# Expert jobs in pairs: 128 places in three passes, then 64 places in two

## The chip, the cores and the metric

The kernel runs on one core of a Trainium2 chip, in one launch. The metric is the device time of that launch in microseconds. Four compute engines matter: TensorE (PE in the profile, its weight loads PEld), VectorE (DVE), ScalarE (ACT) and GpSimd (POOL). SyncE (SP) issues the loads.

## The reference

The reference is a decoder trunk of two layers on 256 tokens of width 1024: an mLSTM layer with a dense SwiGLU, then a sparse attention layer with a mixture of experts, and a last RMSNorm. All is float32. The part that matters here is the mixture:

```python
logits = (t @ w_router)
top_v, top_i = lax.top_k(logits, TOP_K)               # 2 of 8 experts for each token
gate = sum(one_hot(top_i) * softmax(top_v))
gu = einsum('nd,edf->nef', t, w_gu)                   # 1024 -> 2 * 3584 for each expert
act = silu(gu[..., :3584]) * gu[..., 3584:] * gate[..., None]
out = einsum('nef,efd->nd', act, w_down)              # 3584 -> 1024
```

With 256 tokens and two experts each, 512 places are to be filled. On the inputs of the reference its router chooses experts 0 to 7 for 48, 41, 94, 73, 60, 101, 42 and 53 tokens.

## The kernel before

Weights come as slots of 1 MB (128 partitions x 2048 float32), in the order of use: 71 slots for everything ahead of the mixture, then 42 for each expert (28 for gate and up, 14 for down). They pass a ring of 7 raw slots (`RAW`). For float32 precision with the faster fp32r matmul each slot is split: ScalarE copies it to `w_hi` (rounded), VectorE writes `w_lo = raw - w_hi`. Both have a ring of 3 (`SPLIT`). The activations are split in the same way, and TensorE adds three products in `mm3` (lines 1136 to 1138): high x high, high x weight-low, low x weight-high.

So a slot n moves along a chain. SP loads it when VectorE has done slot n-7. ScalarE makes `w_hi` (line 627) when TensorE has used slot n-3. VectorE makes `w_lo` (line 1082). TensorE uses it in 12 matmuls of 128x512 and increments `s_used`. Every engine runs its own instruction list in order, and semaphores tie the lists together.

The mixture runs as jobs in a hardware loop (`Fori(0, jobs)`), one job for each expert with room for 128 places, plus a further job for each expert with more than 128 tokens; with the counts above that is 8 jobs. In a job:

- `gather` (line 1499) picks the tokens of the expert with a one-hot matrix, `gather_t` (line 1514) transposes them, `places` (lines 1505, 1507) makes the gate of each place and the matrix for the way back. They are done for the next job in the down phase of this one.
- Seven chunks of four slots make 512 of the 3584 inner columns each: slots 0 and 1 the gate half in bank 0, slots 2 and 3 the up half in bank 1. ScalarE takes the SiLU into `sg` (line 645), VectorE multiplies with the gate and the up half into `av` (line 1101). In the next chunk `job_t` (line 1547) transposes `av` in four matmuls, ScalarE makes `at_hi` (line 632) and VectorE `at_lo` (line 1089).
- Fourteen down slots accumulate the output in banks 2 and 3. Then `y_hi` (line 661), `y_lo` (line 1112), the scatter back to token order (lines 1594, 1595) and four additions into the residual `xs` (line 1120).

ScalarE and VectorE work `AHEAD` = 2 slots ahead of TensorE in a job, and `TURN` = 3 slots into the next. The table of jobs is made by VectorE ahead of the loop (lines 1033 to 1062), and TensorE, ScalarE, VectorE and SP read the count of jobs from it.

## Time and profile before

| | us |
|---|---|
| median of three runs | 1585.07 (1583.67 to 1586.74) |
| profiled execution, its own time | 1586.67 |
| its span in the profile | 1584.9 |
| TensorE busy | 1536.5 (97%) |
| VectorE busy | 1213.0 (77%) |
| ScalarE busy | 1038.5 (66%) |
| mean load rate over the span | 274 GB/s |

The span runs from the first to the last instruction of the profiled execution. "Idle before" in a row is the time that the engine waited ahead of such instructions, and what ended it. A matmul's duration includes the time in which the next is already running, so the distance between two starts tells the pace, and not the duration.

### The profile page before, as it was taken

The numbers are of one execution on the slowest core, as the hardware profiler recorded it, in microseconds if no ns is written. First come the engines' busy times: TensorE is split into PE (matmuls) and PEld (weight loads), VectorE is DVE, ScalarE is ACT, GpSimd is POOL, SyncE is SP. The second block draws the span as 40 slices with busy tenths as digits, with TensorE's granted clock in tenths as the row PEclk, the third lists the DMA queues.
The fourth block names the chain that finished last, engine by engine and source line by source line (L and its number), as shares of the span: only waits on it lengthen the run. The fifth ranks groups of instructions, "written<-read, shape, count | busy, mean of one in ns | idle before, by whom it ended". The sixth has DMA issues, their size and how long they took to land.

```text
span 1584.9 us, 20492 instructions
## 1 busy us (share of the span) xinstructions
PE 1536.5 (97%) x7380; PEld 1256.4 (79%) x7380; DVE 1213.0 (77%) x1051; ACT 1038.5 (66%) x1006; POOL 38.4 (2%) x92
## 2 busy tenths in 40 slices
PE   7998999999999979999999999999999999999997
PEld 7986888879944668888888887887887887888886
DVE  5945555457458478888988989888988888988887
ACT  5544444346447457777777777777777777777775
POOL 6000000010000000000000000000000000000001
PEclk9998999999959989999999999999999999999999
DMA  8542555535500229989999998998999999998994
GB/s 332 188 158 106 186 187 186 184 134 188 211 1 1 93 102 361 373 329 369 361 348 363 365 352 330 370 360 336 365 360 332 375 351 343 363 365 339 365 359 169
DMA packets 60091, 434.19 MB, mean 274 GB/s; under 512 B 6672, under 2 KB 6672, under 8 KB 7568
## 3 DMA queue, kind: packets, MB, share of 16 engines
q1 hardware_dynamic: 59904, 433.09, 72.5%
q8 instruction: 27, 0.44, 0.1%
q10 hardware_dynamic: 144, 0.52, 0.1%
q14 instruction: 16, 0.13, 0.0%
HBM read 432.54 MB, written 1.05 MB: 274 GB/s over the span
## 4 chain that ended last, share of the span: by engine, by line
PE 93%; DVE 3%; ACT 2%; issue 1%; POOL 0%; DMA 0%; DVEq 0%; POOLq 0%; ACTq 0%
PE bank L1136 27%; PE bank L1138 27%; PE bank L1137 27%; PE bank L1421 2%; PE bank L1447 2%; PE bank L1547 2%; DVE w_lo L1082 1%; PE bank L1499 1%; PE bank L1431 1%; PE bank L1401 1%; PE bank L1449 1%; ACT ht_hi L385 1%; PE bank L1514 0%; DVE w_lo L677 0%; PE bank L1594 0%
## 5 line engine op out<-in xcount | busy, mean ns | idle before, releaser
L1082 DVE TENSOR_TENSOR w_lo<-raw,w_hi 128x2048 fp32r<-128x2048 f32 x336 | 763.3, 2289 | 116.2 <-ACT w_hi L627 115.2
L627 ACT ACTIVATE w_hi<-raw 128x2048 fp32r<-128x2048 f32 x336 | 644.9, 1920 | 161.6 <-PE bank L1138 161.6
L1136 PE MATMUL bank<-w_hi,ht_hi 128*128 128x512 f32 (+1 forms) x1252 | 489.6, 391 | 7.8 <-DVE w_lo L1082 6.1
L1138 PE MATMUL bank<-w_hi,ht_lo 128*128 128x512 f32 (+1 forms) x1252 | 482.9, 386 | 0.0
L1137 PE MATMUL bank<-w_lo,ht_hi 128*128 128x512 f32 (+1 forms) x1252 | 482.4, 385 | 0.0
L1136 PEld LDWEIGHTS bank<-w_hi,ht_hi 128*128 128x128 f32 x1252 | 236.4, 189 | 57.1 <-DVE w_lo L1082 9.6
L1138 PEld LDWEIGHTS bank<-w_hi,ht_lo 128*128 128x128 f32 x1252 | 236.2, 189 | 47.7
L1137 PEld LDWEIGHTS bank<-w_lo,ht_hi 128*128 128x128 f32 x1252 | 236.6, 189 | 44.9
L677 DVE TENSOR_TENSOR w_lo<-raw,w_hi 128x2048 fp32r<-128x2048 f32 x73 | 166.5, 2288 | 128.6 <-ACT w_hi L358 128.6
L358 ACT ACTIVATE w_hi<-raw 128x2048 fp32r<-128x2048 f32 x73 | 139.6, 1919 | 117.1 <-PE bank L1138 116.9
L1136 PE MATMUL bank<-w_hi,at_hi 128*128 128x512 f32 x536 | 211.1, 394 | 0.0
L1138 PE MATMUL bank<-w_hi,at_lo 128*128 128x512 f32 x536 | 209.1, 390 | 0.0
L1137 PE MATMUL bank<-w_lo,at_hi 128*128 128x512 f32 x536 | 208.7, 389 | 0.0
L1138 PEld LDWEIGHTS bank<-w_hi,at_lo 128*128 128x128 f32 x536 | 100.6, 188 | 21.3
L1137 PEld LDWEIGHTS bank<-w_lo,at_hi 128*128 128x128 f32 x536 | 100.8, 188 | 20.2
L1136 PEld LDWEIGHTS bank<-w_hi,at_hi 128*128 128x128 f32 x536 | 100.7, 188 | 20.0
L1136 PE MATMUL bank<-ht_hi,w_hi 128*128 128x256 f32 x256 | 74.2, 290 | 2.7 <-DVE w_lo L677 2.5
L1138 PE MATMUL bank<-ht_hi,w_lo 128*128 128x256 f32 x256 | 73.4, 287 | 0.0
L1137 PE MATMUL bank<-ht_lo,w_hi 128*128 128x256 f32 x256 | 73.4, 287 | 0.0
L645 ACT ACTIVATE sg<-bank 128x512 f32<-128x512 f32 x56 | 33.5, 599 | 42.4 <-PE bank L1138 42.3
L1136 PEld LDWEIGHTS bank<-ht_hi,w_hi 128*128 128x128 f32 x256 | 50.2, 196 | 3.9 <-DVE w_lo L677 2.7
L1137 PEld LDWEIGHTS bank<-ht_lo,w_hi 128*128 128x128 f32 x256 | 50.2, 196 | 0.0
(260 smaller groups left out, 1154.0 us busy)
## 6 DMA issues: line engine op xcount, KB each, us to landing
raw<-in_moe SPq DMA_DIRECT2D x339, 1024.0 KB, 6.9
raw<-in_wts SPq DMA_DIRECT2D x71, 1024.0 KB, 4.8
xs<-in_x SPq DMA_DIRECT2D x2, 512.0 KB, 3.7
out<-xn SPq DMA_DIRECT2D x2, 512.0 KB, 2.7
pk<-in_packed SPq DMA_DIRECT2D x1, 517.0 KB, 6.4
g1b<-in_norm_ffn ACTq DMA_DIRECT2D x1, 512.0 KB, 6.6
gfb<-in_norm_final SPq DMA_DIRECT2D x1, 512.0 KB, 3.7
```

Of the source, the lines that this page charges most:

```text
L358: a(w_hi[:, n % SPLIT, :], raw[:, n % RAW, :], ACT.Copy).then_inc(s_hi, 1)
L385: a(ht_hi[:, k, :], B[banks[b]][:, (k % 2) * 256:(k % 2) * 256 + 256], ACT.Copy, scale=pk[:, C_GAIN + 8 * gain + k:C_GAIN + 8 * gain + k + ...
L627: a(w_hi[:, n % SPLIT, :], raw[:, n % RAW, :], ACT.Copy).then_inc(s_hi, 1)
L645: a(sg[:, 0, :], B[0][:, :], ACT.Silu).then_inc(s_silu, 1)
L677: v.tensor_tensor(w_lo[:, n % SPLIT, :], raw[:, n % RAW, :], w_hi[:, n % SPLIT, :].bitcast(F32), ALU.subtract).then_inc(s_lo, 1)
L1082: v.tensor_tensor(w_lo[:, n % SPLIT, :], raw[:, n % RAW, :], w_hi[:, n % SPLIT, :].bitcast(F32), ALU.subtract).then_inc(s_lo, 1)
L1136: mm(out_, sh, mh, start=first, stop=False)
L1137: mm(out_, sh, ml, start=False, stop=False)
L1138: return mm(out_, sl, mh, start=False, stop=last)
L1421: mm(B[n % 3][:, 0:2 * lk], qt[lo:lo + 64, h // 2, t * P:(t + 1) * P], kt[lo:lo + 64, :, h // R, 0:lk], start=True, stop=True).then_inc(s_ ...
L1447: mm(bank[0:64, :], vv[:, k, b, g * DB:(g + 1) * DB], ptg[grp % 2][:, j, :, :] .rearrange("p r q -> p (r q)"), start=j == 0, stop=False)
L1547: ins = nc.tensor.transpose(B[4 + c % 2][:, j * P:(j + 1) * P], av[:, 0, j * P:(j + 1) * P], ident[:])
```

## The change

Jobs come in pairs. The first of a pair (kind 0) has 128 places and works in three passes as before. The second (kind 1) has 64 places. Its stationary matrix holds the high parts of 64 tokens in columns 0 to 63 and their low parts in columns 64 to 127, so that two matmuls take the place of three: with `w_hi` and with `w_lo`. Rows 0 to 63 of the product are the high part's share and rows 64 to 127 the low part's. They are added by `folded_t`: in place of four transposes of `av`, eight float32 matmuls with a 128x64 matrix `fold` (two identities on top of each other) transpose the gate half and the up half and add the two shares. For that ScalarE copies both halves out of the banks (`sg`, `av`), takes the SiLU after the fold (`silu_t`) and makes the high part (`high_b`), and VectorE multiplies (`product_t`) and makes the low part (`low_b`). ScalarE and VectorE split slots in another order in kind 1, with less lead.

The gate is no longer multiplied in at `av` but at the end of a job, in `y_hi` (a scale for each row) and `y_lo`.

Experts 1 to 7 are sorted by their count. Expert 0 and the three with the highest counts take the jobs of 128 places, the four with the lowest those of 64. A further pair of jobs is made for each expert that has more tokens than its job has places. The table for that is longer; VectorE makes it in the first job, behind the second chunk's product (`job_tables`). The first pair of jobs is written out ahead of the loop, which starts at pair 1. The number of slots and of bytes loaded for each job stays as it was.

```diff
-NJ_MAX = 11
 JOB_SLOTS = 7 * 4 + 14
+PAIRS, PAIRS_MAX = NE // 2, NE // 2 + 4
+CAP_B = 64
...
+    def at_job(i, k, per, plus):
+
+        return i * (2 * per) + (k * per + plus)
...
             load(n, wts[n, :, :])
-        with sp.Fori(0, NE) as i:
+        for s in range(JOB_SLOTS):
...
+        def expert_loads(i, k):
+            if isinstance(i, int):
+                e = sp.value_load(tab[0:1, 1 + 2 * i + k:2 + 2 * i + k], min_val=0, max_val=NE - 1)
+            else:
+                e = sp.value_load(tab[0:1, bass.ds(i * 2 + (1 + k), 1)], min_val=0, max_val=NE - 1)
             for s in range(JOB_SLOTS):
-                load(N0 + s, job_slot(bass.ds(i, 1), s), 1, i * JOB_SLOTS)
-        sp.wait_ge(s_tab, 1)
-        jobs = sp.value_load(tab[0:1, 0:1], min_val=NE, max_val=NJ_MAX)
-        with sp.If(jobs > NE):
-            with sp.Fori(NE, jobs) as i:
-                e = sp.value_load(tab[0:1, bass.ds(i - (NE - 1), 1)], min_val=0, max_val=NE - 1)
-                for s in range(JOB_SLOTS):
-                    load(N0 + s, job_slot(bass.ds(e, 1), s), 1, i * JOB_SLOTS)
+                load(N0 + s, job_slot(bass.ds(e, 1), s), 1, at_job(i, k, JOB_SLOTS, 0))
+
+        expert_loads(0, 1)
+        with sp.Fori(1, pairs) as i:
+            expert_loads(i, 0)
...
+            def silu_t(c):
+                act.wait_ge(s_tp, at_job(i, kind, 7, 11 + c + 1))
+                a(sgt[:, c % 2, :], B[4 + c % 2][:, 0:4 * CAP_B], ACT.Silu).then_inc(s_sgt, 1)
+
+            def high_b(c):
+                act.wait_ge(s_avt, i * 7 + (c + 1))
+                a(at_hi[:, 4 * c * P:(4 * c + 4) * P].rearrange("p (k t) -> p k t", k=4)[:, :, 0:CAP_B],
+                  avt[:, c % 2, :].rearrange("p (k t) -> p k t", k=4), ACT.Copy).then_inc(s_tph, 1)
+
+            split(TURN)
+            if not (isinstance(i, int) and kind == 0):
+                act.wait_ge(s_scat, at_job(i, kind, 4, 0))
+            act.wait_ge(s_gs, at_job(i, kind, 1, 1))
             a(gcol[:], B[6][:, 2 * P:2 * P + 1], ACT.Copy).then_inc(s_gc, 1)
-            split(TURN)
-            act.wait_ge(s_xu, i * 4 + 12)
             a(selt[:], B[6][:, 0:2 * P], ACT.Copy).then_inc(s_sgc, 1)
...
+                    split(4 * c + 3)
+                    if c:
+                        silu_t(c - 1)
+                    used(4 * c + 1)
+                    if c >= 2:
+                        act.wait_ge(s_tp, at_job(i, kind, 7, 11 + c - 1))
+                    a(sg[:, c % 2, :], B[0][:, :], ACT.Copy).then_inc(s_silu, 1)
+                    split(4 * c + 4)
+                    if c:
+                        high_b(c - 1)
+                    split(4 * c + 5)
+                    used(4 * c + 3)
+                    a(av[:, c % 2, :], B[1][:, :], ACT.Copy).then_inc(s_mul, 1)
+                split(28 + 3)
+                silu_t(6)
+                split(28 + 4)
+                high_b(6)
...
+            act.wait_ge(s_gc, at_job(i, kind, 1, 1))
...
-                a(y_hi[:, h * 512:(h + 1) * 512], B[2 + h][:, :], ACT.Copy).then_inc(s_yh, 1)
+                    used(JOB_SLOTS - 1)
+                a(y_hi[:, h * 512:(h + 1) * 512], B[2 + h][:, :], ACT.Copy, scale=gcol[:, 0:1]).then_inc(s_yh, 1)
...
+        def one_hot(j, cap=P):
             for t in range(NT):
-                v.tensor_tensor(sel_oh[:, t, :], slot_iota[:], posj[:, t, j].broadcast_to([P, P]),
+                iota = slot_iota[:, 0:cap].rearrange("p (o n) -> p o n", o=1).broadcast_to([P, P // cap, cap])
+                pos = posj[:, t, j].rearrange("p (o n) -> p o n", o=1).broadcast_to([P, P // cap, cap])
+                v.tensor_tensor(sel_oh[:, t, :].rearrange("p (o n) -> p o n", n=cap), iota, pos,
                                 ALU.is_equal).then_inc(s_sel, 1)
...
+        def job_tables():
...
+            step(v.tensor_tensor(above, above, tie, ALU.add))
+            step(v.tensor_reduce(order, above, AX.X, ALU.add))
+            v.tensor_scalar(large, order, 4.5, None, ALU.is_gt).then_inc(s_dc, 1)
+            v.tensor_scalar(number, order, 2.0, -1.0, ALU.mult, ALU.add).then_inc(s_dc, 1)
+            ch[0] += 2
+            step(v.tensor_scalar(order, order, 0.0, None, ALU.is_equal))
+            step(v.scalar_tensor_tensor(number, large, -7.0, number, ALU.mult, ALU.add))
...
+            step(v.tensor_tensor(large, large, order, ALU.add))
+            step(v.tensor_scalar(cap, large, float(P - CAP_B), float(CAP_B), ALU.mult, ALU.add))
+            step(v.tensor_tensor(over, cnt, cap, ALU.is_gt))
...
+            def spread(table, src, first, n, cols):
+                pick = picks[:, first:first + n, :].rearrange("p (o k) e -> p o k e", o=1).broadcast_to([P, NT, n, NE])
+                work = pwork[:, :, 0:n, :]
+                step(v.tensor_tensor(work, pick, src.rearrange("p t (o e) -> p t o e", o=1)
+                                     .broadcast_to([P, NT, n, NE]), ALU.mult))
+                step(v.tensor_reduce(table[:, :, cols], work, AX.X, ALU.add))
...
+            def product_t(c):
+                dve.wait_ge(s_sgt, i * 7 + (c + 1))
+                if c >= 2:
+                    dve.wait_ge(s_tph, at_job(i, kind, 7, 11 + c - 1))
+                    dve.wait_ge(s_tpl, at_job(i, kind, 7, 11 + c - 1))
+                v.tensor_tensor(avt[:, c % 2, :], sgt[:, c % 2, :], B[4 + c % 2][:, 4 * CAP_B:8 * CAP_B],
+                                ALU.mult).then_inc(s_avt, 1)
+
+            def low_b(c):
+                dve.wait_ge(s_avt, i * 7 + (c + 1))
+                dve.wait_ge(s_tph, at_job(i, kind, 7, 11 + c + 1))
+                both = at_hi[:, 4 * c * P:(4 * c + 4) * P].rearrange("p (k t) -> p k t", k=4)
+                v.tensor_tensor(both[:, :, CAP_B:P], avt[:, c % 2, :].rearrange("p (k t) -> p k t", k=4),
+                                both[:, :, 0:CAP_B].bitcast(F32), ALU.subtract).then_inc(s_tpl, 1)
+
+            if kind == 0:
...
+            else:
+                for c in range(7):
+                    split(4 * c + 2)
+                    if c:
+                        product_t(c - 1)
+                    split(4 * c + 3)
+                    if c:
+                        low_b(c - 1)
+                    split(4 * c + 5)
...
+                product_t(6)
+                split(28 + 4)
+                low_b(6)
+                split(28 + 4 + AHEAD)
...
+                dve.wait_ge(s_yh, at_job(i, kind, 2, h + 1))
+                v.scalar_tensor_tensor(y_lo[:, h * 512:(h + 1) * 512], B[2 + h][:, :], gcol[:, 0:1],
+                                       y_hi[:, h * 512:(h + 1) * 512].bitcast(F32), ALU.mult, ALU.subtract).then_inc(s_yl, 1)
             split(JOB_SLOTS - 1 + AHEAD)
...
-                          kk == 0, kk == 7)
+                if kind == 0:
+                    lo = ht_lo[:, kk // 2, (kk % 2) * P:(kk % 2) * P + P]
+                    ins = mm3(bank[:, :], hi, lo, weights(w_hi, n, 512)[:, k, :], weights(w_lo, n, 512)[:, k, :],
+                              kk == 0, kk == 7)
+                else:
+                    mm(bank[:, :], hi, weights(w_hi, n, 512)[:, k, :], start=kk == 0, stop=False)
+                    ins = mm(bank[:, :], hi, weights(w_lo, n, 512)[:, k, :], start=False, stop=kk == 7)
             ins.then_inc(s_used, 1)
...
+            def folded_t(c):
+                pe.wait_ge(s_silu, at_job(i, kind, 7, 12 + c + 1))
+                pe.wait_ge(s_mul, at_job(i, kind, 7, 12 + c + 1))
+                if c >= 2:
+                    pe.wait_ge(s_avt, i * 7 + (c - 1))
+                for half, src in enumerate((sg, av)):
+                    for j in range(4):
+                        to = (4 * half + j) * CAP_B
+                        ins = mm(B[4 + c % 2][:, to:to + CAP_B], src[:, c % 2, j * P:(j + 1) * P], fold[:],
+                                 start=True, stop=True)
+                ins.then_inc(s_tp, 1)
...
-                    pe.wait_ge(s_silu, i * 7 + 12 + c)
-                    gu(4 * c, B[0], i)
-                gu(4 * c + 1, B[0], i)
+                    pe.wait_ge(s_silu, at_job(i, kind, 7, 12 + c))
+                    gu(4 * c, B[0], i, kind)
+                    if kind:
+                        folded_t(c - 1)
+                gu(4 * c + 1, B[0], i, kind)
                 if c:
-                    job_t(c - 1)
-                    pe.wait_ge(s_mul, i * 7 + 12 + c)
+                    if kind == 0:
+                        job_t(c - 1)
+                    pe.wait_ge(s_mul, at_job(i, kind, 7, 12 + c))
...
+                            ins = mm3(B[2 + half][:, :], hi, at_lo[:, kk * P:(kk + 1) * P],
+                                      weights(w_hi, n, 1024)[:, k, w], weights(w_lo, n, 1024)[:, k, w], first, last)
+                        else:
+                            mm(B[2 + half][:, :], hi, weights(w_hi, n, 1024)[:, k, w], start=first, stop=False)
+                            ins = mm(B[2 + half][:, :], hi, weights(w_lo, n, 1024)[:, k, w], start=False, stop=last)
                     if d == 13 and half == 0:
...
+        job(0, 0)
+        job(0, 1)
+        pe.wait_ge(s_tab, 1)
+        pairs = pe.value_load(tab[0:1, 0:1], min_val=PAIRS, max_val=PAIRS_MAX)
+        with pe.Fori(1, pairs) as i:
+            job(i, 0)
+            job(i, 1)
 
```

## Rows read from the trace of the kernel before

**Rows 1.** First section of the page.

```profile
PE 1536.5 (97%) x7380; PEld 1256.4 (79%) x7380; DVE 1213.0 (77%) x1051; ACT 1038.5 (66%) x1006; POOL 38.4 (2%) x92
```

**Rows 2.** Windows; columns: length, busy time of each engine, granted clock, DMA share, GB/s.

```profile
6.00:32.00 26.00, 22.18 (x155) 21.23 (x156) 17.96 (x24) 13.04 (x19) 20.24 (x49) 0.93 1.01 416
588.00:1570.00 982.00, 975.75 (x4453) 805.59 (x4452) 860.71 (x520) 738.35 (x521) 0.00 (x0) 1.00 0.92 351
```

**Rows 3.** The tile selt: one such copy in each job.

```profile
L640 ACT ACTIVATE selt<-bank x8: 360/385/388, 584.1 to 1451.7; 128x256 fp32r<-128x256 f32 x8
```

**Rows 4.** Timeline of TensorE in a chunk; columns: start, duration in us, what.

```profile
1019.25 0.39 PE L1136 MATMUL bank<-w_hi,ht_hi 128*128 128x512 f32 x1
...
1025.14 0.39 PE L1138 MATMUL bank<-w_hi,ht_lo 128*128 128x512 f32 x1
1025.37 0.60 PE L1547 MATMUL bank<-ident,av 128*128 128x128 f32 x4
1025.72 0.47 PE L1136 MATMUL bank<-w_hi,ht_hi 128*128 128x512 f32 x1
```

**Rows 5.** Groups by line and shape, window 620 to 1540 (busy us, mean ns, idle before).

```profile
L1082 DVE TENSOR_TENSOR w_lo<-raw,w_hi 128x2048 fp32r<-128x2048 f32 x312 | 708.7, 2289 | 103.7 <-ACT w_hi L627 102.7
L627 ACT ACTIVATE w_hi<-raw 128x2048 fp32r<-128x2048 f32 x312 | 599.0, 1920 | 148.0 <-PE bank L1138 148.0
...
L1089 DVE TENSOR_TENSOR at_lo<-bank,at_hi 128x512 fp32r<-128x512 f32 x54 | 36.9, 683 | 0.0
L632 ACT ACTIVATE at_hi<-bank 128x512 fp32r<-128x512 f32 x54 | 32.1, 594 | 9.9 <-PE bank L1547 9.9
...
L645 ACT ACTIVATE sg<-bank 128x512 f32<-128x512 f32 x52 | 31.1, 599 | 39.8 <-PE bank L1138 39.7
...
L1505 PEld LDWEIGHTS bank<-gatej,sel_oh 128*128 128x128 f32 x32 | 4.8, 190 | 0.7
...
L990 DVE TENSOR_TENSOR sel_oh<-slot_iota,posj 128x128 fp32r<-128x128 f32 x16 | 3.9, 284 | 0.0
```

**Rows 6.** Timeline of TensorE: float32 matmuls of the places.

```profile
1041.79 0.50 PE L1505 MATMUL bank<-gatej,sel_oh 128*128 x4
1042.15 0.42 PE L1507 MATMUL bank<-ident,sel_oh 128*128 128x128 f32 x2
```

**Rows 7.** Timeline of VectorE at the turn of two jobs.

```profile
701.70 0.69 DVE L1112 TENSOR_TENSOR y_lo<-bank,y_hi 128x512 fp32r<-128x512 f32 x1 [0.23 <-ACT y_hi L661]
702.31 2.28 DVE L1082 TENSOR_TENSOR w_lo<-raw,w_hi 128x2048 fp32r<-128x2048 f32 x1
704.51 2.47 DVE L1120 TENSOR_TENSOR xs<-xs,bank 128x512 f32<-128x512 f32 x4
706.90 6.68 DVE L1082 TENSOR_TENSOR w_lo<-raw,w_hi 128x2048 fp32r<-128x2048 f32 x3
```

**Rows 8.** Timeline of VectorE: two dependent small steps of the router.

```profile
572.20 0.17 DVE L1021 SCALAR_TENSOR_TENSOR rt<-rt 128x16 f32<-128x16 f32 x1
572.41 0.17 DVE L1022 TENSOR_SCALAR posj<-rt 128x16 f32<-128x16 f32 x1
```

**Rows 9.** Timeline of TensorE: two idle times, each ahead of the matmul shown.

```profile
16.68 0.39 PE L1136 MATMUL bank<-ht_hi,w_hi 128*128 128x256 f32 x1 [2.48 <-DVE w_lo L677]
...
569.87 0.39 PE L1486 MATMUL bank<-rt,tri 128*128 128x8 f32 x2 [2.28 <-DVE rt L1012]
```

**Rows 10.** Windows behind those idle times, and one with a shorter gap.

```profile
16.00:18.00 2.00, 1.31 (x10) 1.32 (x11) 2.00 (x2) 1.91 (x2) 1.78 (x3) 0.96 1.05 442
18.00:20.00 2.00, 2.00 (x12) 2.00 (x11) 2.00 (x2) 0.00 (x0) 1.91 (x2) 0.50 0.97 410
20.00:22.00 2.00, 2.00 (x14) 2.00 (x14) 1.03 (x1) 0.00 (x0) 1.75 (x4) 0.69 1.05 438
394.00:395.00 1.00, 0.32 (x3) 0.32 (x4) 1.00 (x2) 1.00 (x3) 0.00 (x0) 1.00 0.00 0
570.00:572.00 2.00, 1.36 (x10) 1.26 (x10) 2.00 (x3) 0.00 (x0) 0.00 (x0) 0.70 0.00 0
```

More of the change, by code:

```diff
@@ L337, in _ @@
                                  base=t * P, pattern=[[-1, T]], channel_multiplier=1))
+        step(g.memset(fold[:], 0.0))
+        for first in (0, CAP_B):
+            step(g.affine_select(out=fold[:], in_=fold[:], compare_op=ALU.not_equal, fill=1.0, base=-first,
+                                 pattern=[[-1, CAP_B]], channel_multiplier=1))
         step(g.memset(xf[:, XW - 12:XW], 0.0))
@@ L1021, in _ @@
         step(v.scalar_tensor_tensor(rf[6], rf[6], 1.0, rf[5], ALU.add, ALU.mult))
[L1022 removed]
+        step(v.tensor_scalar(posj[:, :, 0:1], r[6][:, :, 0:1], -1.0, None, ALU.add))
         one_hot(slice(0, 1))
```

303 lines of the change are left out of this document (180 added, 123 removed).

## The prediction

> **What bounds the kernel now.** I read the busy times first [rows 1]: TensorE 97%, VectorE 77%, ScalarE 66%. Then the long windows [rows 2]: in the mixture TensorE works 975.75 of 982 us at the full clock, and loads run at 351 GB/s. The tile `selt` dates the jobs: eight copies, the first at 584.1, the last at 1451.7, so 867.6 / 7 = 123.9 us for each job [rows 3]. The groups [rows 5] then say who follows whom: ScalarE's splits wait for TensorE (148.0 us), VectorE's for ScalarE (102.7 us), and TensorE is the pace. From 1019.25 to 1025.14 there are 26 matmuls, 0.2265 us each, and four transposes cost 0.35 us [rows 4]. A slot of 12 matmuls is 2.72 us, a chunk 48 x 0.2265 + 0.4 = 11.3 us. But VectorE is close behind: a split takes 2.29 us alone and (6.68 - 2.28) / 2 = 2.20 us back to back [rows 5, 7].
>
> **What two passes remove.** A slot of a 64-place job is 8 x 0.2265 = 1.81 us of TensorE. Over 42 slots that is 38 us less for each such job, 152 us for the four of them, if TensorE stayed the bound. It doesn't: 42 splits of VectorE are 42 x 2.20 = 92 us, with its other work some 105. And below that stands the chain through the order of the lists, so I work out the time from that.
>
> **A chunk in two passes.** From the end of `w_lo` of a chunk's first slot to the same point of the next chunk, each step waits for the one before: TensorE slot 0, 1.81; `folded_t`; slot 1, 1.81; the last matmul's end, 0.39 - 0.23 = 0.17 behind its pace. Then ScalarE: the copy `sg` (0.60), the split of the next chunk's first slot (it has to wait for slot 1 too, by the ring of 3), 1.92, and `high_b`. Then VectorE: `low_b`, which stands ahead of that slot's split, and the split, 2.29. Back-to-back work on ScalarE and VectorE overlaps by 0.09 (2.29 - 2.20) at each of three places, and I take 0.04 for each of three changes of engine (0.02 to 0.1, estimated: it is small beside the rows).
>
> The parts that no row shows: `high_b` has 256 columns from SBUF; a ScalarE copy of 256 columns is 0.385 [rows 3], of 512 is 0.594 [rows 5]. I take 0.40. `low_b` and `product_t` of 256 columns on VectorE lie between 0.284 (128 columns) and 0.683 (512) [rows 5]: a straight line gives 0.42. `folded_t` is 8 float32 matmuls; the two float32 products of the places show as 4 records in 0.36 us [rows 6], two records each at 0.09, so 16 records are 1.44, and I take 1.6. At least it is 8 transposes, 8 x 0.09 = 0.7 [rows 4]; at most 16 weight loads of 0.19 one after the other, 3.0 [rows 5].
>
> Sum: TensorE 1.81 + 1.6 + 1.81 + 0.17 = 5.39; ScalarE 0.60 + 1.92 + 0.40 - 0.18 = 2.74; VectorE 0.42 + 2.29 - 0.09 = 2.62; changes 0.12. Together **10.9 us a chunk, against 11.3 now**. So the gate and up stage, two thirds of the slots, gains next to nothing. VectorE's own work in a chunk is 4 x 2.20 + 0.8 = 9.6 and ScalarE's 9.0, below the chain. TensorE works 4 x 1.81 + 1.6 = 8.8 and stands idle for 2.1 us, in one gap ahead of slot 0. With `folded_t` at 0.7 a chunk is 10.0, with 3.0 it is 12.3.
>
> **The down stage.** Here VectorE is the pace. From the `w_lo` of slot 28 to that of slot 2 of the next job are 16 splits, 35.2 us. Beside them stand the one-hot (0.5), `product_t` and `low_b` (0.8), the gathered low parts (1.3), `y_lo` (1.3) and the additions (2.4, as 704.51 to 706.90 [rows 7]), together 6.3, and some 1.7 of waits: for `silu_t` behind the fold, for the gathered rows, for `y_hi`. That is 43.2 us.
>
> **The job.** It starts with two splits (4.4 us, to slot 4), then six chains (6 x 10.9 = 65.4), then 43.2: **113.0 us against 123.9, 10.9 less, 44 us for four jobs.** A 128-place job keeps its 123.9: its slots are 12 matmuls as before, and its last part, from the end of slot 41 to slot 2 of the next job, is VectorE's list (`y_lo` at 701.70, split, additions, split to 709.2 [rows 7]), which doesn't shorten when slots 0 and 1 behind it do.
>
> **What is added.** `job_tables`: some 25 steps that each wait for the one before, 0.21 each [rows 8], and a dozen that don't, together about 7 us on VectorE in the first job, between the product of the second chunk and the split of slot 10. TensorE has slots 8 and 9 ready then, with the transposes 5.9 us of work; the product, the tables and the split of slot 10 take 0.7 + 7 + 2.2 = 9.9. So TensorE stands still for 4 us, and I add 1.5 for the clock behind it: 5.5, between 0 (the lead is larger) and 9 (the steps take half as long again). The old tables, 2.7 us ahead of the loop, lay beside the gathering, and their going gives nothing. The scale in `y_hi` and the gate in `y_lo` lengthen a path at each of eight turns by at most 0.1 to 0.2 us: 1. At the end of a two-pass job TensorE waits about 2.8 us for the split behind the additions, which has its price in the clock (below), 1.5 at three turns: 4.5. Work that costs nothing: `fold` on GpSimd, which is idle there (38 us busy in all [rows 1]); the loads' wait for the table on SP's queue, a job of loads behind it, with five slots landed ahead; the ScalarE copies of `gcol` and `selt`, hidden behind splits that were made ahead.
>
> Without anything from the clock in the chunks: 44 - 5.5 - 1 - 4.5 = **33 us less**.
>
> **The clock.** TensorE's clock stood at 0.50, its lower level of 1.2 GHz, after idle times like the new ones: idle 2.48 us ahead of 16.68, and the windows from 16 to 22 show 0.96, 0.50 and 0.69, some 3.4 us at the lower level; idle 2.28 ahead of 569.87, and 0.70 in the window from 570. At 394 with 0.68 of a microsecond idle it stayed at 1.00 [rows 9, 10]. In 3.4 us at half rate TensorE loses 1.7 us of work, and in a chunk that falls on slot 0, the fold and slot 1, all on the chain. There are 24 gaps of 2.1 us. Both gaps with a fall had thin work around them, these have dense work for 8.8 us between them, so I expect a fall behind about half: 12 x 1.7 = 20 us.
>
> **The loads.** A pair of jobs takes 88.1 MB in 123.9 + 113.0 = 237 us, 372 GB/s. The trace shows 416 GB/s over 26 us at the start [rows 2], so loads don't bind; over the short stretch where VectorE splits at 2.2 us a slot (477 GB/s for 8 slots) the ring's lead covers the difference. The Trainium skill says otherwise ("DMA: Bandwidth & Descriptors", section "Where 436 GB/s comes from"): for loads from HBM the core's share of about 358 GB/s binds, not the 435 of the fabric. By that rule a pair would take 246 us, against 247.8 now, and the change would give next to nothing; the trace's 416 GB/s, with the chip's other cores idle, speaks against it.
>
> **The numbers and the rivals.** Against the profiled execution's 1586.7, which lies 1.6 above the median:
>
> 1. *Forecast: chain-bound chunks, and a fall of the clock behind half of the gaps.* 33 - 20 = 13 less: 1573.7, in terms of the median **1572**. Its own range is 1562 to 1582. Chance 0.40.
> 2. *The same, and no falls in the chunks*: the dense work between the gaps holds the clock. 1552. For it: TensorE is busy for 80% of a chunk. With the fold at its lower bound it is 24 x 0.9 = 22 less, 1530. Chance 0.31.
> 3. *A fall behind every gap* (the two rows of idle times both had one): 24 x 1.7 = 41 against the 33: 1593, slower than before. It turns at 19 of the 24 gaps. Chance 0.10. A fold at its upper bound does the same without the clock: 24 x 1.4 = 34 back, 1586 with no falls. Chance 0.07.
> 4. *The loads bind* at the rate that now goes with the mixture (351 at a share of 0.92, so 382 at most): a pair then takes 231, below the 237 of the chain, no loss. Only at 358 or below would nothing be left, 1586. Chance 0.03.
> 5. *A two-pass job isn't what it seems*: an expert of a 64-place job has more than 64 tokens, and a pair of jobs is added, 237 us more. The four lowest counts of experts 1 to 7 are 41, 42, 53 and 60, so four pairs suffice. Chance 0.02.
> 6. *The lists interlock better than I followed them*, VectorE's 105 us as the whole job: 19 x 4 = 76 less, minus 11: 1520. Against it: `low_b` waits for `high_b`, which stands behind a split. Chance 0.07.
>
> Range 1546 to 1594. Less than 0.2% (3.2 us) is what a measurement of this kernel can't tell from no change. Faster: cases 2, 6 and most of 1, 0.77. Slower: case 3, half of the long fold, case 5, the edge of case 1, 0.15. Same: 0.08.
>
> **What would show it.** In the new trace the distance between two firsts of four splits in a 64-place job should be 10.9 us (12.6 where the clock fell), with `low_b` right behind `high_b` and the next split right behind that, and one gap of 2.1 us of TensorE ahead of each chunk's slot 0. `folded_t` should take 1.6 us. VectorE should be gapless from slot 35 to 42. 64-place jobs should take 113 to 119 us and 128-place jobs 124. VectorE's tables should take 7 us, TensorE's standstill there 4. The granted clock in windows of the 64-place jobs tells cases 1 to 3 apart. I am wrong if the chunk isn't chain-bound (VectorE gapless in it), if the loads show ScalarE's splits waiting for them, or if the 128-place jobs change by more than a microsecond or two.

## The result, and the profile after

The changed kernel takes 1599.6 us (median of 4 runs, 1595.2 to 1604.5) against 1585.0 for the kernel before beside it (1583.7 to 1586.7): ratio 1.0087, 95% interval 1.0066 to 1.0109. It is slower by 0.9%; 1572 was forecast, and the range ended at 1594. (Ratios here are as recorded; they differ from the quotient of two medians by about 0.002 at most.) The profiled execution took 1604.5 us (span 1602.7), 17.8 more than the one of before.

From the page of the kernel after: busy times, the granted clock in 40 slices, the shares of the chain that ended last, and three groups (line, engine, tiles, count | busy us, mean ns | idle us ahead and who ended it).

```profile
PE 1483.2 (93%) x7044; PEld 1193.8 (74%) x7044; DVE 1194.6 (75%) x1074; ACT 1028.0 (64%) x1047; POOL 39.0 (2%) x95
PEclk9998999999958999999899999999999899999989
PE 76%; DVE 12%; ACT 5%; issue 5%; POOL 0%; DMA 0%; DVEq 0%; ACTq 0%; POOLq 0%
L1191 DVE TENSOR_TENSOR w_lo<-raw,w_hi 128x2048 fp32r<-128x2048 f32 x336 | 759.2, 2286 | 87.2 <-ACT w_hi L650 87.1
L650 ACT ACTIVATE w_hi<-raw 128x2048 fp32r<-128x2048 f32 x336 | 641.5, 1915 | 156.5 <-PE bank L1291 93.0
L1684 PE MATMUL bank<-w_hi,ht_hi 128*128 128x512 f32 x448 | 191.3, 427 | 46.6 <-DVE w_lo L1191 45.9
```

TensorE's busy share fell from 97% to 93% [rows 1], yet the span grew. No engine is the pace any more: VectorE still waits for ScalarE's splits and ScalarE for TensorE [rows 5], and now TensorE waits for VectorE too, 45.9 us ahead of the two-pass gate and up matmuls (L1684). Each of those takes 427 ns in the mean, where one at full clock takes 0.39: many ran at half rate.

By windows from one job's scatter to the next (columns: stretch, length, busy us and count of PE, PEld, DVE, ACT, POOL, granted clock, DMA share, GB/s). The first two windows hold a 64-place and a 128-place job, the next two likewise, the last a 64-place job:

```profile
714.74:839.29 124.55, 108.40 (x483) 85.86 (x482) 104.72 (x67) 93.95 (x79) 0.00 (x0) 0.93 0.91 346
839.29:962.89 123.60, 122.38 (x559) 100.96 (x558) 107.34 (x67) 89.93 (x65) 0.00 (x0) 1.00 0.94 366
962.89:1084.95 122.06, 106.85 (x483) 84.40 (x482) 104.92 (x67) 94.08 (x79) 0.00 (x0) 0.94 0.91 344
1084.95:1212.31 127.36, 123.81 (x559) 102.07 (x558) 107.10 (x67) 89.90 (x64) 0.00 (x0) 0.99 0.94 364
1212.31:1337.62 125.31, 110.22 (x484) 87.10 (x483) 104.92 (x67) 94.19 (x79) 0.00 (x0) 0.92 0.88 336
```

A job took 124.1 us before. A 64-place job now takes 122.1 to 125.3, with its clock at 0.92 to 0.94; a 128-place job takes 123.6, or 127.4 where a turn of the loop lies in it. The 17.8 us are made up so:

| part of the profiled execution | forecast, us | measured, us |
|---|---|---|
| ahead of the first gather | 0 | +3.6 |
| first job (tables) | +5.5 | +7.5 |
| three 128-place jobs | some +0.5 | +5.9 |
| four 64-place jobs | -44 + 4.5 + 20 + some 0.5 | +0.7 |
| behind the last scatter | 0 | +0.1 |

The first row is no effect of the change: in the profiles of the eleven kernels below, which have the same code there, the first gather starts between 567.3 and 576.0 (573.3 in the kernel before, 576.9 in the changed one).

The gaps of TensorE in the first 64-place job, from its timeline (start, us, engine, line, tiles, [idle before, ended by]; other rows are left out), windows around three of them, and windows from one gap's end to the next:

```profile
721.54 0.62 PE L1684 MATMUL bank<-w_hi,ht_hi 128*128 128x512 f32 x1 [2.57 <-DVE w_lo L1191]
...
738.10 0.47 PE L1684 MATMUL bank<-w_hi,ht_hi 128*128 128x512 f32 x1 [1.58 <-DVE w_lo L1191]
...
749.48 0.47 PE L1684 MATMUL bank<-w_hi,ht_hi 128*128 128x512 f32 x1 [2.03 <-DVE w_lo L1191]
...
760.79 0.47 PE L1684 MATMUL bank<-w_hi,ht_hi 128*128 128x512 f32 x1 [1.98 <-DVE w_lo L1191]
...
772.12 0.47 PE L1684 MATMUL bank<-w_hi,ht_hi 128*128 128x512 f32 x1 [1.98 <-DVE w_lo L1191]
...
785.06 0.47 PE L1684 MATMUL bank<-w_hi,ht_hi 128*128 128x512 f32 x1 [1.98 <-DVE w_lo L1191]
...
799.49 0.50 PE L1768 MATMUL bank<-w_hi,at_hi 128*128 128x512 f32 x1 [1.89 <-DVE w_lo L1191]
```

```profile
762.00:764.00 2.00, 2.00 (x17) 1.85 (x15) 2.00 (x2) 1.04 (x2) 0.00 (x0) 1.00 1.01 360
...
772.00:774.00 2.00, 1.88 (x6) 1.59 (x7) 2.00 (x1) 1.33 (x1) 0.00 (x0) 0.72 0.96 397
774.00:776.00 2.00, 2.00 (x9) 1.71 (x8) 2.00 (x2) 0.70 (x1) 0.00 (x0) 0.50 0.89 356
...
785.00:787.00 2.00, 1.94 (x8) 1.62 (x9) 2.00 (x1) 1.27 (x1) 0.00 (x0) 0.89 0.78 221
787.00:789.00 2.00, 2.00 (x11) 1.90 (x9) 2.00 (x2) 1.37 (x1) 0.00 (x0) 0.50 0.94 377
```

```profile
760.79:772.12 11.33, 9.35 (x49) 7.72 (x49) 9.65 (x7) 8.98 (x9) 0.00 (x0) 1.00 1.01 365
772.12:785.06 12.94, 10.96 (x49) 9.04 (x49) 9.65 (x7) 9.09 (x9) 0.00 (x0) 0.87 0.91 360
785.06:799.49 14.43, 12.54 (x48) 10.44 (x48) 9.55 (x7) 8.99 (x9) 0.00 (x0) 0.76 0.85 310
```

The gap of 2.57 us is ahead of the job's slot 2, the next five are ahead of chunks 2 to 6, the last is ahead of slot 28, the first of the down stage. A fall here is a stretch in which the granted clock is at 0.50. A chunk without one is 11.31 us long (749.48 to 760.79). Three gaps of the same 1.98 us follow. Behind the first the clock stays at 1.00; behind the second and third it falls, and the chunks are 12.94 and 14.43 us long, 1.6 and 3.1 more. The granted clock of 0.87 and 0.76 over these chunks makes 3.4 and 6.9 us at the lower level. So a fall of 3.4 us costs 1.6 us, and some falls last twice as long and cost twice as much.

The chain of one chunk on VectorE and ScalarE, from the two engines' timelines:

```profile
754.19 2.28 DVE L1191 TENSOR_TENSOR w_lo<-raw,w_hi 128x2048 fp32r<-128x2048 f32 x1
758.01 0.43 DVE L1212 TENSOR_TENSOR at_hi<-avt,at_hi 128x256 fp32r<-128x256 f32 x1 [1.54 <-ACT at_hi L666]
758.36 4.49 DVE L1191 TENSOR_TENSOR w_lo<-raw,w_hi 128x2048 fp32r<-128x2048 f32 x2
```

```profile
755.21 0.60 ACT L695 ACTIVATE sg<-bank 128x512 f32<-128x512 f32 x1 [1.39 <-PE bank L1685]
755.71 1.91 ACT L650 ACTIVATE w_hi<-raw 128x2048 fp32r<-128x2048 f32 x1
757.51 0.40 ACT L666 ACTIVATE at_hi<-avt 128x256 fp32r<-128x256 f32 x1
```

`sg` waits for slot 1; behind it stand the split and `high_b`; VectorE is idle for 1.54 us until `high_b` ends, does `low_b`, and only then the split that TensorE waits for, done at 760.64.

### The profile page after: what moved, and what is told of

Read it like the earlier page. It is cut to its first block, busy times and chain, and to the rows that moved or that the text cites. A ratio compares the mean times of both kernels' runs of the same rounds, so it can differ in the third digit from the quotient of the medians.

```text
span 1602.7 us, 19559 instructions
## 1 busy us (share of the span) xinstructions
PE 1483.2 (93%) x7044; PEld 1193.8 (74%) x7044; DVE 1194.6 (75%) x1074; ACT 1028.0 (64%) x1047; POOL 39.0 (2%) x95
## 3 DMA queue, kind: packets, MB, share of 16 engines
q8 instruction: 62, 1.02, 0.3%
## 4 chain that ended last, share of the span: by engine, by line
PE 76%; DVE 12%; ACT 5%; issue 5%; POOL 0%; DMA 0%; DVEq 0%; ACTq 0%; POOLq 0%
PE bank L1289 17%; PE bank L1291 17%; PE bank L1290 17%; DVE w_lo L1191 9%; PE bank L1684 4%; PE bank L1685 4%; PE bank L1715 4%; ACT w_hi L650 3%; PE bank L1574 2%; PE bank L1600 2%; PE bank L1652 1%; PE bank L1584 1%; PE bank L1768 1%; PE bank L1769 1%; PE bank L1554 1%
## 5 line engine op out<-in xcount | busy, mean ns | idle before, releaser
L1289 PE MATMUL bank<-w_hi,ht_hi 128*128 128x512 f32 (+1 forms) x804 | 315.3, 392 | 16.2 <-DVE w_lo L1191 7.4
L1291 PE MATMUL bank<-w_hi,ht_lo 128*128 128x512 f32 (+1 forms) x804 | 310.1, 386 | 0.0
L1290 PE MATMUL bank<-w_lo,ht_hi 128*128 128x512 f32 (+1 forms) x804 | 310.0, 386 | 0.0
L1684 PE MATMUL bank<-w_hi,ht_hi 128*128 128x512 f32 x448 | 191.3, 427 | 46.6 <-DVE w_lo L1191 45.9
L1289 PEld LDWEIGHTS bank<-w_hi,ht_hi 128*128 128x128 f32 x804 | 153.8, 191 | 49.5 <-issue 16.4
L1685 PE MATMUL bank<-w_lo,ht_hi 128*128 128x512 f32 x448 | 186.7, 417 | 0.0
L1291 PEld LDWEIGHTS bank<-w_hi,ht_lo 128*128 128x128 f32 x804 | 153.4, 191 | 30.6
L1290 PEld LDWEIGHTS bank<-w_lo,ht_hi 128*128 128x128 f32 x804 | 153.9, 191 | 28.4
L1684 PEld LDWEIGHTS bank<-w_hi,ht_hi 128*128 128x128 f32 x448 | 90.0, 201 | 78.4 <-DVE w_lo L1191 45.7
L1289 PE MATMUL bank<-w_hi,at_hi 128*128 128x512 f32 x312 | 122.6, 393 | 0.0
L1291 PE MATMUL bank<-w_hi,at_lo 128*128 128x512 f32 x312 | 121.6, 390 | 0.0
L1290 PE MATMUL bank<-w_lo,at_hi 128*128 128x512 f32 x312 | 121.4, 389 | 0.0
L1768 PE MATMUL bank<-w_hi,at_hi 128*128 128x512 f32 x224 | 95.2, 425 | 14.6 <-DVE w_lo L1191 12.5
L1685 PEld LDWEIGHTS bank<-w_lo,ht_hi 128*128 128x128 f32 x448 | 90.4, 202 | 18.3
```

Source lines behind the costliest of these rows:

```text
L1289: mm(out_, sh, mh, start=first, stop=False)
L1290: mm(out_, sh, ml, start=False, stop=False)
L1291: return mm(out_, sl, mh, start=False, stop=last)
L1684: mm(bank[:, :], hi, weights(w_hi, n, 512)[:, k, :], start=kk == 0, stop=False)
L1685: ins = mm(bank[:, :], hi, weights(w_lo, n, 512)[:, k, :], start=False, stop=kk == 7)
L1768: mm(B[2 + half][:, :], hi, weights(w_hi, n, 1024)[:, k, w], start=first, stop=False)
```

## The experiments

Each ratio is to the kernel before, run on the same chip. The theory: (a) the order of the lists puts `low_b` ahead of a split that TensorE needs, which makes a gap of 2 us in each chunk; (b) the gap brings falls of the clock; (c) the tables in one piece cost what the first job lost; (d) the loop's turn, with two jobs in its body, costs 3.5 us. The rivals are that the two-pass form itself doesn't pay, and that loads bind.

**e1_fill**: the gaps filled with matmuls that nobody reads.

```
+ def filler(n): n matmuls of ht_hi into bank 3
  pe.wait_ge(s_yl, ...); filler(9)     # kind 1, behind slot 1 of the job
  filler(7)                            # kind 1, behind slot 3 of chunks 1 to 6
```

> The changed kernel with TensorE kept busy in its gaps: in the 64-place jobs, seven matmuls of 128x512 (1.6 us) into the then unused bank 3 behind slot 3 of chunks 1 to 6, and nine behind slot 1 ahead of slot 2. Nothing else changes. Theory (the clock): the two-pass chunk is a chain of 11.2 us, and the gaps of 1.8 to 2.5 us in it let the clock fall to its lower level; 64-place jobs show a mean granted clock of 0.92 to 0.94, some 21 falls at 1.6 us each. With the gaps filled the granted clock in those jobs is 1.00, every chunk takes 11.2 us and the time falls by 25 to 34 us, to 1566 to 1575. Rival (the lists alone): the extra length of the chunks comes from how the three engines' lists interlock, the clock only falls because TensorE waits; then filling brings nothing or costs a little, 1598 to 1605.

**e2_order**: `low_b` one split later on VectorE's list.

```
-                    split(4 * c + 3)
+                    split(4 * c + 4)
                     if c:
                         low_b(c - 1)
```

> The changed kernel with low_b moved behind the split of the next chunk's first slot in VectorE's list (64-place jobs). Theory (the chain): low_b waits for high_b, and the split behind it waits too; taken off the chain the chunk falls from 11.2 to about 10.5 us, TensorE's gap from 1.8 to 1.1, which is too short for the clock to fall: 24 x 0.75 = 18 and most of 34 us for the clock, so 1550 to 1565. If only the chain shortens and the clock falls as before: 1580 to 1585. Rival (VectorE itself is the bound of these jobs): nothing changes, 1597 to 1602.

e1_fill: 1570.8 us, ratio 0.9907 (0.9875 to 0.9938). e2_order: 1556.9 us, ratio 0.9821 (0.9796 to 0.9846). A 64-place job of each, from the windows (e1_fill, then e2_order), and a gap of e2_order:

```profile
950.07:1066.58 116.51, 112.38 (x535) 88.85 (x533) 104.78 (x67) 93.80 (x79) 0.00 (x0) 1.00 0.94 363
```

```profile
947.66:1060.34 112.68, 101.05 (x483) 79.07 (x482) 104.36 (x67) 93.82 (x79) 0.00 (x0) 1.00 0.94 371
```

```profile
990.49 0.50 PE L1684 MATMUL bank<-w_hi,ht_hi 128*128 128x512 f32 x1 [1.15 <-DVE w_lo L1191]
...
1001.05 0.50 PE L1684 MATMUL bank<-w_hi,ht_hi 128*128 128x512 f32 x1 [1.14 <-DVE w_lo L1191]
```

Parts (a) and (b) of the theory are shown. The fillers do no useful work and leave the chain as it is (chunks of 11.20 and 11.33 us), and a 64-place job falls from 124.3 (mean) to 116.7 us with the clock at 1.00: the clock's falls cost 7.6 us a job, 30 us in all. In e2_order the same matmuls wait 1.15 us instead of 1.98, a chunk is 10.56 us, no fall follows any of these gaps without a filler, and the job takes 112.7 to 113.9. Two of its four 64-place jobs (113.9 and 113.5 us) still have one fall, behind the gap of 2.5 us ahead of slot 2, which this edit leaves. One line moved is worth 2.6%.

**e3_three** and **e3b_three**: the 64-place jobs worked in three passes, without the fold. In e3_three my edit made the tables a second time, in the second job. That costs time there and leaves wrong places, so the kernel's output is wrong; e3b_three makes them once.

```
-            if kind == 0:            # VectorE's, ScalarE's and TensorE's lists, and mm3
+            if True:
```

> The changed kernel with the 64-place jobs worked as 128-place jobs in three passes (no fold, no two passes); the new tables, the sorting, the gate at the end, the pairs and the loop stay. It tells what the two passes alone gave. Theory: the two-pass jobs gave nothing, they take 122 to 125 us as the three-pass ones do, so this runs at 1594 to 1602, and what it has above the kernel before comes from the tables (7 us) and the turns of the loop (3.7 us each for two turns). Rival (the two passes give the 11 us a job that the sum had, and something else eats it): then this is slower than the change by 30 to 44 us, 1630 to 1644.

> The changed kernel with the 64-place jobs worked as the 128-place ones: three passes, three matmuls for each of the blocks, no fold, the places sorted and paired and the scales' tables as in the change, and the loop over pairs kept. This time the tables are made once. Theory: two passes with falls of the clock cost as much as three without: the 64-place jobs take 124.2 to 124.4 us each at clock 1.00 against 124.3 in the mean in the changed kernel, the two loop turns cost 3.3 to 3.6 us each as before, and the whole is within 3 us of the changed kernel: ratio to the kernel before 1.006 to 1.010. Rival: the two-pass form itself gains even with its falls (by 5 us or more), then this kernel is slower than the changed one, at 1.012 or more, as the first try with three passes (1.0159) would say if the second making of its tables had cost nothing.

e3_three: 1611.8 us, ratio 1.0159 (1.0138 to 1.018). e3b_three: 1604.8 us, ratio 1.0113 (1.0078 to 1.0148). Two windows of e3b_three, a 64-place job and a 128-place job with a turn in it:

```profile
961.48:1085.76 124.28, 123.26 (x563) 101.76 (x562) 108.51 (x67) 91.10 (x64) 0.00 (x0) 1.00 0.92 350
1085.76:1213.66 127.90, 125.11 (x563) 102.85 (x562) 108.62 (x67) 90.76 (x64) 0.00 (x0) 0.99 0.92 350
```

The jobs came out as the theory had them: 124.3 us in three passes at full clock, 124.3 in the mean in two passes with the falls. The whole lies 0.0013 above the range that I expected, and its interval holds the changed kernel's 1.0087, so the runs show no gain of the two passes as they were written. The table step costs about 9 us where it stands alone: 133.1 against 124.3 in e3_three's second job.

**e4_unroll** and **e8_peout**: the loop over pairs written out, on all engines and on TensorE alone. (Every kernel with a written-out loop serves four pairs, the number that these counts need, and leaves out the further ones that the loop would serve.)

```
-        with pe.Fori(1, pairs) as i:
+        for i in range(1, PAIRS):
             job(i, 0)
             job(i, 1)
```

> The changed kernel with the four pairs written out one after the other, no hardware loop (the count of pairs is taken as four, which it is on these inputs). Theory (the turn of the loop): at two of the turns TensorE starts slot 1 of the next job 3.4 to 3.6 us late with nothing to wait for, since the body of a pair is twice as long as the loop was before, and the clock falls behind it; the 128-place jobs behind a turn take 127.3 instead of 123.6. Without turns: 7 to 8 us less, 1591 to 1593. Rival (the length of the program, not the turn): the idle times stay and come at other places, 1597 to 1603.

> The changed kernel with TensorE's loop over pairs written out (four pairs, the number that these counts need; a fifth, that the loop would serve, is left out); ScalarE, VectorE and SyncE keep their loops. Theory: the 3.3 to 3.6 us in which PE stands still for nothing that the profile shows are PE's own turn of a loop body that its instruction memory doesn't hold whole. Without it the 128-place jobs with a turn in them take 123.4 to 124 us instead of 127.4, with no row of PE of over 1 us <-issue, and the whole falls by 6 to 8 us: ratio 1.003 to 1.006 (0.003 of luck of the clock in the 64-place jobs either way). Rival: another engine's turn holds PE up (VectorE's split of a slot comes late behind its own turn): the jobs stay at 127 us and PE's idle time is then ended by w_lo.

e4_unroll: 1599.1 us (1588.0 to 1608.5), ratio 1.0078 (1.0046 to 1.0109). e8_peout: 1594.4 us, ratio 1.0077 (1.0041 to 1.0113). The first matmul of slot 1 behind the turn, of the changed kernel, of e4_unroll and of e8_peout, and the 128-place job of e8_peout:

```profile
1090.53 0.79 PE L1289 MATMUL bank<-w_hi,ht_hi 128*128 128x512 f32 x1 [3.55 <-issue]
```

```profile
1091.90 0.47 PE L1292 MATMUL bank<-w_hi,ht_hi 128*128 128x512 f32 x1 [1.07 <-DVE w_lo L1193]
```

```profile
1090.13 0.47 PE L1289 MATMUL bank<-w_hi,ht_hi 128*128 128x512 f32 x1 [0.97 <-DVE w_lo L1191]
```

```profile
1084.38:1207.67 123.29, 122.32 (x559) 100.98 (x558) 107.03 (x67) 89.91 (x64) 0.00 (x0) 1.00 0.96 374
```

In the changed kernel TensorE stands for 3.55 us with no engine to blame ("issue"), and its next matmuls take 0.63 us each, the lower clock. With only TensorE's loop written out this is gone, and the job takes 123.3 instead of 127.4: the cause is TensorE's own turn. What in the turn takes the time (the fetch of instructions, or another thing) no run here separates. The whole didn't follow: the 6 to 8 us that I expected are less than the luck of the clock. In e8_peout one 64-place job took 128.9 us at a clock of 0.89, another 121.4 at 0.96, with the same instructions. Neither kernel's total tells it from the changed one. Where the gaps of 2 us are gone, the turn does show in the total: e7_all (0.9658) and e10_foldtab (0.9721), both below, differ in the written-out loop alone, and their intervals only touch, at 0.9686.

**e5_tables**: the tables in five pieces.

```
-                    if c == 1 and isinstance(i, int):
-                        job_tables()
+                    if 1 <= c <= 5 and isinstance(i, int):
+                        next(making, None)       # job_tables cut by four yields
```

> The changed kernel with one edit: the making of the scales' tables (job_tables) is cut into five pieces, one behind the product of each of the chunks 1 to 5 of the first job, instead of 7 us of small steps in one row on VectorE. Theory: the first job's 5.7 us of PE gap and the fall of the clock behind it go, the first job takes 130.5 to 131.5 us instead of 137.8, the rest is as it was: 6 to 7 us off the whole, a ratio to the kernel before of 1.003 to 1.006 where the changed kernel has 1.0087 (the clock's luck in the 64-place jobs moves it by 0.003 either way). Rival: the tables' steps aren't what the first job lost (the gather's lists and the first 64-place hand-over are), and five small gaps cost as much as one: first job still 136 to 138 us, ratio 1.008 to 1.010.

1595.6 us, ratio 1.0045 (1.0014 to 1.0075). The matmul ahead of which TensorE stood in the changed kernel's first job, the windows of that stretch there, and the same windows of e5_tables:

```profile
617.59 0.77 PE L1289 MATMUL bank<-w_hi,ht_hi 128*128 128x512 f32 x1 [5.67 <-DVE w_lo L1191]
```

```profile
612.00:618.00 6.00, 0.41 (x1) 0.44 (x2) 5.62 (x17) 2.40 (x3) 0.00 (x0) 0.82 0.01 5
618.00:622.00 4.00, 4.00 (x11) 3.03 (x11) 4.00 (x3) 0.00 (x0) 0.00 (x0) 0.50 0.86 295
```

```profile
612.00:618.00 6.00, 6.00 (x30) 4.94 (x29) 5.86 (x11) 4.45 (x5) 0.00 (x0) 1.00 0.91 345
```

In e5_tables no gap of over 0.4 us is left behind the first gather (570.2) up to there, and the first job takes 131.3 us from gather to scatter, against 137.9 (130.3 in the kernel before). Part (c) of the theory holds: 6.6 us.

**e6_foldlate**: the fold behind slot 1 instead of slot 0, and what hangs on it one split later on ScalarE's list and two later on VectorE's.

```
 PE:   gu(slot 0); [-folded_t(c-1)]; gu(slot 1); [+folded_t(c-1)]; gu(slot 2); ...
 ACT:  split(+3); sg; split(+4); [+silu_t]; split(+5); [+high_b]
 DVE:  split(+4); [+product_t]; split(+5); [+low_b]
```

> The changed kernel with the fold and all that hangs on it put later: TensorE folds a chunk behind the next chunk's slot 1 instead of behind its slot 0; ScalarE does silu_t behind the split of slot 4 ahead and high_b behind the next, VectorE product_t and low_b likewise. Theory (the chain fold, silu_t, high_b, product_t, low_b, split makes the 2 us gap, and the gap makes the clock fall): the gap ahead of a chunk's slot 0 falls below 0.9 us, the clock stays at 1.00 in the 64-place jobs, a chunk takes 10.0 to 10.2 us (VectorE has 9.6 us of work in it, and 4.19 MB take 10.1 us at the 416 GB/s of rows 2), a 64-place job 110 to 111.5 us, the whole a ratio of 0.972 to 0.978. First rival, loads: at 397 GB/s (what the kernel with low_b moved behind the next split reached, 10.56 us a chunk at a DMA share of 0.99) the transfers are already at their end, and this kernel is no faster than that one: chunk 10.5 us, ratio 0.981 to 0.984, with PE's gaps ended by w_lo or w_hi that wait for their loads. Second rival: the later fold moves the wait to the first down slot of the job, which is 2 us later: 64-place jobs 112 to 113 us.

1541.2 us (1539.5 to 1548.3), ratio 0.9728 (0.9694 to 0.9762). From its timelines, two gaps of TensorE, then VectorE's list through a chunk; and a 64-place job by window:

```profile
994.71 0.50 PE L1683 MATMUL bank<-w_hi,ht_hi 128*128 128x512 f32 x1 [0.70 <-DVE w_lo L1191]
...
1004.79 0.50 PE L1683 MATMUL bank<-w_hi,ht_hi 128*128 128x512 f32 x1 [0.71 <-DVE w_lo L1191]
```

```profile
992.36 2.29 DVE L1191 TENSOR_TENSOR w_lo<-raw,w_hi 128x2048 fp32r<-128x2048 f32 x1 [0.47 <-ACT w_hi L650]
994.57 0.42 DVE L1212 TENSOR_TENSOR at_hi<-avt,at_hi 128x256 fp32r<-128x256 f32 x1
994.95 6.69 DVE L1191 TENSOR_TENSOR w_lo<-raw,w_hi 128x2048 fp32r<-128x2048 f32 x3
1001.56 0.41 DVE L1205 TENSOR_TENSOR avt<-sgt,bank 128x256 f32<-128x256 f32 x1
1002.45 2.29 DVE L1191 TENSOR_TENSOR w_lo<-raw,w_hi 128x2048 fp32r<-128x2048 f32 x1 [0.48 <-ACT w_hi L650]
```

```profile
940.32:1050.51 110.19, 102.31 (x484) 80.47 (x482) 104.62 (x67) 93.83 (x79) 0.00 (x0) 0.98 0.95 381
```

The chunk is 10.08 us and VectorE idle for 0.47 of it: now VectorE is nearly the pace. No fall follows a gap of 0.7 us; the clock of 0.98 is that of one fall behind the gap ahead of slot 2, which three of the four 64-place jobs still have. 4.19 MB in 10.08 us are 416 GB/s, the rate of [rows 2], sustained in the midst of the mixture, so loads did not bind at 397 either.

**e7_all** (late fold, tables in pieces, loop written out), **e9_turn** (that, and nine unread matmuls behind slot 1 of each 64-place job) and **e10_foldtab** (late fold and tables, the loop kept):

```
 e9_turn:  + if kind and c == 0: pe.wait_ge(s_yl, ...); filler(9)
```

> The fold put later as in e6_foldlate, the tables in five pieces as in e5_tables, and the loop over pairs written out, so that no engine takes a loop turn. Theory: the three add up: 64-place jobs 110 to 111.5 us, first job 131, 128-place jobs 123.5 us: some 1530 us on the scale of a kernel before of 1585, a ratio of 0.963 to 0.969. Rival: the instructions of the written-out loop come from memory anyway and cost as much as the turns, or the loads take back what the turns gave: ratio as e6_foldlate less the tables' 0.004, 0.969 to 0.975.

> The kernel e7_all with nine matmuls more, whose result nobody reads, behind slot 1 of each 64-place job, where TensorE waits 2.5 us for the split of slot 2. Theory: this last long gap brings the one fall of the clock that the 64-place jobs still have (granted 0.98 in three of four of them); filled, the clock stays at 1.00 and a 64-place job takes 109.5 to 110 us instead of 109.6 to 111.1: 1 to 4 us off the whole, ratio 0.963 to 0.966 where e7_all has 0.9658. Rival: the fillers delay slot 2's own matmuls by a few tenths each and the fall comes elsewhere: no gain, 0.965 to 0.968.

> The fold put later (e6_foldlate) and the tables in five pieces (e5_tables), the loop over pairs kept, so that the kernel still serves counts that need a fifth pair. Theory: the tables' 6.6 us come off the 1541 us of e6_foldlate: 1534 to 1536 us on the scale of a kernel before of 1586, ratio 0.967 to 0.970. Rival: with the denser chunks the pieces hit VectorE, which has 9.6 of 10.1 us of work, but the first job is a 128-place one, where VectorE has 13 per cent free: if it is late anyway, the first job takes 134 us or more and the ratio stays at 0.972.

e7_all: 1532.9 us, ratio 0.9658 (0.963 to 0.9686). e9_turn: 1528.9 us, 0.9655 (0.962 to 0.969). e10_foldtab: 1541.0 us, 0.9721 (0.9686 to 0.9757). A 64-place job of e7_all and of e9_turn:

```profile
1173.95:1285.03 111.08, 102.15 (x483) 80.52 (x482) 104.18 (x67) 93.82 (x79) 0.00 (x0) 0.98 0.97 387
```

```profile
1169.41:1279.30 109.89, 103.11 (x493) 80.93 (x492) 104.14 (x67) 93.84 (x79) 0.00 (x0) 1.00 0.97 392
```

e7_all adds up as expected and beats the kernel before by 3.4%. In e9_turn the last fall of the clock in a 64-place job is gone, for 1.2 us in that job, and all four take 109.8 to 109.9; the ratio can't tell the two kernels apart. e10_foldtab missed its expected ratio, 0.967 to 0.970: its first job is 131.4 us against 138.1 in e6_foldlate, yet the medians are the same. Its rival had the same ratio, but with a first job of 134 us or more, and that isn't what happened. Its profiled execution had its first gather 8.7 us later (576.0 against 567.3), in code that the two share. Whether the runs differ so as well, no run here shows.

## Why the prediction was wrong

**Right.** The chain, step by step: `low_b` directly behind `high_b`, the next split directly behind that, and six gaps in a 64-place job, ahead of chunks 2 to 6 and of slot 28, of 1.5 to 2.0 us (2.1 forecast); the two splits at the start, 4.4 us; `folded_t` 1.70 us (740.01 to 741.71 in the timeline, 1.6 taken); `high_b` 0.40 and `low_b` 0.42; the tables' 7 us on VectorE (608.2 to 615.1). Loads bound nowhere and no pair was added. "A fall behind about half" held too: windows from each of the 24 gaps to the next show one behind 14 of them, where I had 12, at 1.6 us (1.7). So rival 3, a fall behind every gap, is not what happened; that its 1593 lies nearest to the result is luck.

**The step that failed: "113.0 us against 123.9, 10.9 less, 44 us for four jobs".** With the clock held at 1.00 a 64-place job takes 116.5 to 117.4 us (e1_fill), 7.4 less in the mean than the 124.1 of before, and not 10.9. That is 30 us for four jobs instead of 44, the largest error of the sum, and it comes from two of its terms:

- "10.9 us a chunk": a chunk without falls is 11.2 to 11.3 us. A change of engine is 0.10 to 0.15, not 0.04 (slot 1's end to `sg`, `high_b` to `low_b`, the split to the matmul), and the fold 0.1 longer. The gate and up stage thus gained nothing over the 11.3 of three passes. The six chains took 67.3 to 68.0 us in e1_fill, not 65.4.
- "That is 43.2 us", the down stage: from the `w_lo` of slot 28 to that of the next job's slot 2 it is 43.9 to 44.2 us in e1_fill. In the changed kernel it is 45.4 to 45.8, with the 1.6 us of a fall behind the gap ahead of slot 28 in it. Besides the wait for `silu_t`, VectorE stands for ScalarE's splits, here in the second 64-place job of the changed kernel:

```profile
1051.16 0.42 DVE L1205 TENSOR_TENSOR avt<-sgt,bank 128x256 f32<-128x256 f32 x1 [1.14 <-ACT sgt L662]
...
1054.59 2.29 DVE L1191 TENSOR_TENSOR w_lo<-raw,w_hi 128x2048 fp32r<-128x2048 f32 x1 [0.80 <-ACT w_hi L650]
...
1058.74 4.49 DVE L1191 TENSOR_TENSOR w_lo<-raw,w_hi 128x2048 fp32r<-128x2048 f32 x2 [1.53 <-ACT w_hi L650]
```

Those are 3.5 us of waits, with the fall. In e1_fill's first 64-place job, without it, the same three places have 0, 0.51 and 1.49 us, and 0.73 for `y_hi` comes to them: 2.7 where I had summed 1.7. The two terms are 2.6 to 3.6 us a job; the rest of the difference is that the windows run from scatter to scatter and the sum from split to split.

**The clock: 30 us, against 24.5 forecast for chunks and turns.** The places where the clock was low sum to 72 us in the four 64-place jobs (length times twice what the granted clock lacks to 1), as long as 21 falls of 3.4 us. They are 18 falls: 14 in the chunks, three of them twice as long, so 17 times 1.6 or 27 us where I had 20, and one at each of the four gaps ahead of slot 2, for the other 3. I had taken 3.4 us for every fall. That the second of my two examples lasted longer, windows behind the one that [rows 10] shows would have told: from 572 to 576 the clock stood at 0.50, and at 0.59 from 576 to 578. The gap at the turn of two jobs was forecast at the end of a two-pass job, three times, of 2.8 us. At the one of these places where no turn of the loop lies it is 1.2 us, without a fall; a gap of 2.5 us is at the start of each two-pass job instead, behind slot 1.

**The first job.** VectorE's 7 us were right, TensorE's standstill was 5.67 us instead of 4, and the clock stayed down for more than 4 us behind it: 7.5 in all, not 5.5. From the product's start (607.57) the product, the tables and the split took 10.0 us, as forecast, but TensorE had work only until 611.92: 4.35 us of lead, where I had counted the whole 5.9 of slots 8 and 9. It had begun on them before VectorE began on the product.

**What was not in the sum: the loop's turn.** I costed each part of the body and not the body's length. The turn stands where slot 1 of a 128-place job begins, 3.3 to 3.6 us of idle time and a fall, twice: those jobs are 3.1 to 3.3 us longer than the 124.1 of before, and 4 us longer than with TensorE's loop written out (e8_peout). Before, the turn was there seven times and cost nothing that [rows 3] would show.

The account closes: against the forecast of 13 less, 64-place jobs 20 worse (14 of it the chain's and the down stage's, 5.8 the clock's), turns 5.4, first job 2, the head 3.6, together 31, and 30.8 were measured. No single term takes the time out of the range; their sum does. The deeper mistake stands ahead of all terms: the chain was laid open in the prediction itself, with `low_b` ahead of the split that TensorE waits for. Rival 6 said that VectorE's 105 us a job is the floor if the lists interlock, 1520; it needed another list, and with that list 1541 came.

## What to carry to other kernels

When a pass is taken from the engine that sets the pace, follow the chain through the in-order lists of the engines that feed it, and place what nobody waits for yet (`low_b`) behind what somebody does (the split), in the same edit. Count a gap of two microseconds on TensorE as its own length and, in 14 of 24 cases here, a fall of the clock; the same gap cut to 1.15 us cost only itself. When a loop's body doubles, look at the turn by itself: here it cost nothing with 563 matmuls in the body and some 4 us with 1042.
